# Stick-breaking iterations in two slices, with three PSUM banks for turned weights and one for outputs

## The reference

```python
def _stick_breaking(q, k, v, q_pos, k_pos):
    z = jnp.einsum('bqhd,bkhd->bhqk', q, k) * (SB_HEAD_DIM ** -0.5)
    causal = k_pos[None, :] < q_pos[:, None]
    log_keep = jnp.where(causal, jax.nn.log_sigmoid(-z), 0.0)
    after = lax.cumsum(log_keep, axis=3, reverse=True) - log_keep
    a = jnp.where(causal, jnp.exp(jax.nn.log_sigmoid(z) + after), 0.0)
    o = jnp.einsum('bhqk,bkhd->bqhd', a, v)
```

## Time and profile before

| | us |
|---|---|
| median of 3 runs | 1417.03 (1416.87 to 1417.48) |
| the profiled execution, its own time | 1415.79 |
| its span | 1414.0 |
| PE busy in the span | 1364.6 (97%) |
| DVE busy | 1000.3 (71%) |
| ACT busy | 624.1 (44%) |
| stick-breaking iterations 20 to 39 | about 436 to 582 |

### The profile page before, as it was taken

The page is one execution under the profiler, slowest core; times in us unless marked ns, Lnnn a source line. Parts: engine busy times, 40 slices in busy tenths (PEclk is TensorE's granted clock), DMA queues, the critical chain, the costliest instruction groups (busy, mean ns, idle before and its releaser), DMA issues. The chain is left out here.

```text
span 1414.0 us, 23804 instructions
## 1 busy us (share of the span) xinstructions
PE 1364.6 (97%) x9152; PEld 1195.7 (85%) x9152; DVE 1000.3 (71%) x1319; ACT 624.1 (44%) x1112; POOL 451.9 (32%) x412
## 2 busy tenths in 40 slices
PE   6999999989999999899789999999999999999997
PEld 5778888768888777688689999999999998788886
DVE  5896858598877999656677766666766567754466
ACT  6634333278887877323352222222222233533343
POOL 2133331010010000111164543544554454644344
PEclk9999999989999999999999999999999999999999
DMA  7265542455544555433234533444533448854554
GB/s 249 75 212 189 203 156 73 145 153 143 139 119 121 138 146 147 147 120 108 67 120 144 173 113 136 158 144 144 174 126 132 149 158 284 304 176 163 164 182 171
DMA packets 172200, 218.05 MB, mean 154 GB/s; under 512 B 19836, under 2 KB 110328, under 8 KB 170680
## 3 DMA queue, kind: packets, MB, share of 16 engines
q1 hardware_dynamic: 163416, 193.13, 41.9%
q0 software_dynamic: 3840, 12.58, 2.7%
q10 hardware_dynamic: 4832, 10.82, 2.1%
HBM read 152.98 MB, written 63.50 MB: 153 GB/s over the span
## 5 line engine op out<-in xcount | busy, mean ns | idle before, releaser
L792 PE MATMUL ps_proj<-shared 128*128 128x512 f32 x224 | 90.0, 402 | 2.4 <-DVE shared L546 1.5
L2605 ACT COPY aux<-ps_feed 128x544 f32<-128x544 f32 x22 | 13.5, 612 | 170.3 <-PE ps_feed L2926 170.3
L793 PE MATMUL ps_proj<-shared 128*128 128x512 f32 x224 | 87.9, 392 | 0.0
L794 PE MATMUL ps_proj<-shared 128*128 128x512 f32 x224 | 87.9, 392 | 0.0
L2555 POOL TENSOR_TENSOR ring_more<-staging,ring_more 128x512 fp32r<-128x512 f32 x45 | 69.5, 1548 | 56.5 <-ACT ring_more L2591 56.4
L2555 POOL TENSOR_TENSOR shared<-staging,shared 128x512 fp32r<-128x512 f32 x41 | 60.0, 1468 | 86.1 <-ACT shared L2591 86.1
L1408 ACT COPY aT<-ps_aT 128x512 f32<-128x512 f32 (+2 forms) x168 | 81.1, 526 | 10.7 <-PE ps_aT L1735 9.6
L1735 PE MATMUL ps_aT<-ident,z 128*128 128x128 f32 (+1 forms) x568 | 83.5, 280 | 1.9 <-DVE z L1580 1.7
L2819 DVE TENSOR_TENSOR blocks<-ps_feed,blocks 128x512 f32<-128x512 f32 x56 | 35.9, 681 | 67.1 <-PE ps_feed L2955 67.1
L1580 DVE TENSOR_TENSOR_SCAN z<-z,near 128x1024 f32<-128x1024 f32 (+7 forms) x64 | 81.4, 1335 | 0.0
L2924 PE MATMUL ps_feed<-shared,ring_more 128*128 128x272 f32 x264 | 76.6, 290 | 2.4 <-issue 2.4
(11 more groups left out here) (364 smaller groups left out, 4527.1 us busy)
## 6 DMA issues: line engine op xcount, KB each, us to landing
staging<-s_dram SPq DMA_DIRECT2D x50, 256.0 KB, 4.2
staging<-in_w_gate SPq DMA_DIRECT2D x11, 1024.0 KB, 7.8
blocks<-in_w_up SPq DMA_DIRECT2D x11, 1024.0 KB, 5.4
blocks<-in_w_down SPq DMA_DIRECT2D x11, 1024.0 KB, 9.8
t_dram<-blocks SPq DMA_DIRECT2D x11, 1024.0 KB, 3.9
s_dram<-blocks SPq DMA_DIRECT2D x11, 1024.0 KB, 5.2
w_raw<-in_w_in SPq DMA_DIRECT2D x10, 1024.0 KB, 6.5
staging<-in_cache_sb_v POOLq DMA_DIRECT2D x31, 256.0 KB, 3.2
```

The source lines that it names most:

```text
L792: nc.tensor.matmul(res, a_hi[:, k, cols], b_hi[:, k], start=start, stop=False)
L793: nc.tensor.matmul(res, a_hi[:, k, cols], b_lo[:, k], start=False, stop=False)
L794: return nc.tensor.matmul(res, a_lo[:, k, cols], b_hi[:, k], start=False, stop=(k == HK - 1))
L2605: nc.scalar.copy(two(first), bank(u, 0)).then_inc(first_done, 1)
```

## The change

In stick-breaking iterations (i >= 20) all engines use the slices `((0, 1, 2), (3, 4), ())`: three groups are turned in a row, then all products that are due follow in one row, then three score units; then two groups, their products and the rest of the units, and both pieces of preparation. The products run three groups behind instead of two. For this the four PSUM banks beside the ring are dealt out anew: three for turned groups and one for outputs in stick-breaking steps (differential ones keep two and two). A turned group then waits for the copy of the group three before, and the first product of a step for the output of the step just before. The ring for the scores keeps its four banks. No operation is added or removed.

```diff
-    RAW, RING, ZS, AT, LAG, POS = 6, 4, 4, 4, 2, 5
+    RAW, RING, ZS, AT, POS = 6, 4, 4, 4, 5
-    SLICES = ((0, 1), (2, 3), (4,))
+    DIFF_SLICES, SB_SLICES = ((0, 1), (2, 3), (4,)), ((0, 1, 2), (3, 4), ())
+    def slices(i):
+        return SB_SLICES if i >= SB0 else DIFF_SLICES
+    def lag(x):
+        return 2 if is_diff(x) else 3
     def pieces_of(i, s):
+        if i >= SB0:
+            return prep_at.get(i, ()) if s == 1 else ()
         return prep_at.get(i, ())[s - 1:s] if s else ()
+    def turned_bank(x, g):
+        G = grp0[x] + g
+        return G % 2 if is_diff(x) else (G - grp0[SB0]) % 3
+    def output_bank(x):
+        return 2 + x % 2 if is_diff(x) else 3
...
-        ps_aT = psum("ps_aT", [P, 2, 4, P])
-        ps_o = psum("ps_o", [P, 2, BANK])
+        ps_w = psum("ps_w", [P, 4, BANK])
...
-                if G >= 2:
-                    pe.wait_ge(a_copied, G - 1)
+                first = grp0[SB0]
+                if is_diff(x) or G < first + 2:
+                    if G >= 2:
+                        pe.wait_ge(a_copied, G - 1)
+                elif G == first + 2:
+                    pe.wait_ge(o_done, SB0 - 1)
+                else:
+                    pe.wait_ge(a_copied, G - 2)
...
-                        pe.wait_ge(o_done, x - 1)
+                        pe.wait_ge(o_done, x - 1 if is_diff(x) else x)
...
+            valued = upto = 0
             for i in iterations:
-                for s, slots in enumerate(SLICES):
+                for s, slots in enumerate(slices(i)):
                     turned_now = [j for j in slots if 0 <= i < NSTEP and j < len(groups(i))]
                     for j in turned_now:
                         turn(i, j)
-                    for j in turned_now:
-                        if grp0[i] + j >= LAG:
-                            values(grp0[i] + j - LAG)
-                    for j in slots:
-                        if i == NSTEP and j < LAG:
-                            values(len(owner) - LAG + j)
+                    if turned_now:
+                        upto = grp0[i] + turned_now[-1] + 1 - lag(i)
+                    elif i == NSTEP:
+                        upto = len(owner)
+                    while valued < upto:
+                        values(valued)
+                        valued += 1
                     for j in slots:
                         if 0 <= i + SCORE < NSTEP and j < len(units(i + SCORE)):
                             score(i + SCORE, j)
```

More of the change, by code:

```diff
@@ L1407, in collect @@
                 f = sum(m == P for _, _, _, _, m in bl)
-                last = nc.scalar.copy(aT[:, G % AT, 0:f], ps_aT[:, G % 2, 0:f])
+                ps = ps_w[:, turned_bank(x, g)].rearrange("p (k n) -> p k n", n=P)
+                last = nc.scalar.copy(aT[:, G % AT, 0:f], ps[:, 0:f])
                 if f < len(bl):
                     m = bl[f][4]
-                    last = nc.scalar.copy(aT[0:m, G % AT, f], ps_aT[0:m, G % 2, f])
+                    last = nc.scalar.copy(aT[0:m, G % AT, f], ps[0:m, f])
                 last.then_inc(a_copied, 1)
@@ L1420, in output @@
                     act.wait_ge(v_last_loaded[u % 2], 32 * ((u - ND) // 2 + 1))
-                o, ps = o_sb[:, x % 4], ps_o[:, x % 2]
+                o, ps = o_sb[:, x % 4], ps_w[:, output_bank(x)]
                 if is_sample(x) and is_diff(x):
@@ L1731, in turn @@
                     pe.wait_ge(ready, ready0[x] + 2 * r + h + 1)
-                if G >= 2:
-                    pe.wait_ge(a_copied, G - 1)
+                first = grp0[SB0]
[6 more added lines that the diff above has]
+                    pe.wait_ge(a_copied, G - 2)
+                ps = ps_w[:, turned_bank(x, g)].rearrange("p (k n) -> p k n", n=P)
                 for k, (_, _, _, at, m) in enumerate(groups(x)[g]):
-                    last = nc.tensor.transpose(ps_aT[0:m, G % 2, k], z(x, at, m), t["ident"][:, :])
+                    last = nc.tensor.transpose(ps[0:m, k], z(x, at, m), t["ident"][:, :])
                 last.then_inc(a_turned, 1)
@@ L1758, in values @@
                     val = v[u % 2][0:m, (NB if is_sample(x) else 0) + k]
-                    out = ps_o[:, x % 2]
+                    out = ps_w[:, output_bank(x)]
                     if is_diff(x):
```

## The result

The changed kernel takes 1422.95 us (1421.66 to 1424.89, 6 runs) against 1417.14 (1416.57 to 1417.95, 6 runs) of the kernel before on the same chip: a ratio of 1.0044 [1.0034, 1.0054], slower by 5.8 us. The profiled execution took 1421.66 us, its span is 1419.9. The prediction said 1422.2.

A forecast was written before the change was run, and what follows sets the result against it. PE, busy 97% of the span, was taken as the bound, with DVE close behind. DVE's last stretch 5.4 us later, less 0.3, plus 0.1 gave 1421.0 profiled; the median standing 1.24 higher, 1422.2 us, range 1417.6 to 1426.0.

The forecast's parts named there:

- The wait: In 14 prompt-scoring iterations PE's third score unit waits for ACT's sigmoids to free the first unit's banks, 0.8 to 1.1 us each.
- the 6 us under which I would have been wrong: Sign against the forecast: PE's idle time on scores under 6 us, where some 13 us was expected.
- The savings: Joined runs on PE save 0.14 (transposes) and 0.18 us (products) in each of 20 iterations, plus score-run ends.
- no wait to speak of: Rival: banks come free in time and only savings remain, 8.9 us on PE, of which DVE leaves part; 1412 us, 9%.
- The sum: Waits of 10.4 us less savings through iteration 32 bring PE 4.4 us later to iteration 33; the span grows by 5.2 us.
- the saving of 0.42: Per prompt-scoring iteration on PE: 0.32 us from joined transposes and products plus 0.10 for one end of a score run.
- The tail: DVE's last stretch, from the last preparation piece to the last scan, sets the stage's end and starts 5.4 us later.
- One output bank: A step's first product waits for the previous output; covered by scores, and in iterations 37 to 39 at worst 0.1 us each.
- The hole of 0.27 us: Wait in the transposes starting iteration 24, for an older group's copy; gone with three banks, the same taken for 29 and 34.
- The scans: Rival: DVE's scans come too late for the third group in iterations like 26, 31, 36; 2.8 us more, 1425.0 us, 14%.
- The clock: Rival: PE's clock falls to 1.2 GHz behind each of the 14 waits; 25 us more, 1447 us, 2%.

The follow-up runs named there:

- e2: The kernel before, with only the third score unit moved to join the first two in slice 0; 1425.76 us, ratio 1.0067.
- e1: The changed kernel, with the third score unit back in the second slice, behind the transposes and products of groups 3 and 4; 1415.08 us, ratio 0.9992.
- e3: The changed kernel, with the score units of each prompt step from step 23 on sorted by width, narrowest first; 1418.34 us, ratio 1.0013.
- e10: The kernel before, with only the new bank deal: three banks for turned groups, one for outputs in stick-breaking steps; 1416.48 us, ratio 0.9997.
- e5: The kernel of e1, with the rounding and remainder of the output weights moved from DVE to POOL; 1417.97 us, ratio 1.0008.
- e4: The changed kernel, with two banks for turned groups and two for outputs as before, products still three groups behind; 1434.04 us, ratio 1.0122.

## Why the prediction was right

**The wait, right.** Third units start 2.28 or 2.29 us after first ones of 512 (iterations 25, 26), and 1.89 where the first unit has 384 (23, 28; forecast 1.87). The sum of the idle marks is 11.2 us in 14 waits (13.4 by starts), all in the iterations and at the units that were named; the 6 us under which I would have been wrong were far off. e2 shows that the order of the units alone makes them, e1 that they go with it, e3 that their size follows the width of the first unit.

**The savings, right.** 12 transposes take 1.40 us (forecast 1.46), 20 products 1.24 (1.23). e1 is the kernel that has the savings without the wait: its stage is 2.24 us shorter. So they are there, but the rival "no wait to speak of" had the right reason against itself: of 8.9 us on PE most is not to be had, because DVE is next. It took half to two thirds as what remains, 5 us; a quarter (2.24 of 8.9) is what remained.

**The sum, 1.1 us short.** Through iteration 32 the change costs 5.10 us by lengths of iterations, against 4.4. By type of iteration (x mod 5 = 0, 1, 2, 3) the prediction gave 0.53, 0.70, 0.37 and 0.47 more for each with prompt scores, and 0.69 less for 24 and 29. Measured: 0.56 and 0.54 in 25 and 30 (but 0.12 in 20, the first of the stage), 0.87, 0.97 and 0.98 in 21, 26 and 31, 0.48, 0.48 and 0.47 in 22, 27 and 32, 0.48 in 23 and 28, and 0.67 and 0.65 less. The step that failed in size is the saving of 0.42, above all in the iterations with x mod 5 = 1, where it was 0.15 in 26 and 31. In 26 the wait is what was forecast, 1.12 (from 486.00 + 0.12 to 487.24); but the third unit's run had been followed at once by two small transposes of preparation before, which cost nothing extra at its end, so that no end was saved there, and the 12 transposes at the start took 1.51 us, 0.11 over those of iteration 25. I used the rows of iteration 25 for all, and 26 had another order behind its third unit. In 22, 27 and 32 the saving was 0.31: the sample step's products (L1764 before, L1788 after) gave 0.06 instead of 0.18. Against that stands luck of 0.4 in iteration 20, which nobody had forecast: with the longer lag 8 recorded products fewer are due there (28 instead of 36), and they come back behind the last transposes of the stage.

**The tail, right in kind.** DVE's last stretch sets the end: 34.03 us long in both. By the distance from iteration 20 it starts 6.06 us later, not 5.4, which is the same 0.7 as above. From the last scan to `mix` the sum had 0.2 less, and it is 0.2 more: that is the other 0.4 of the 1.1. "One output bank" was the other undersized term: nothing before iteration 37, as said, but 0.28 there and 0.39 at the last step, where I had at worst 0.1 each. e10, where the products are two groups behind, has neither.

**The rest.** The hole of 0.27 us is gone in the changed kernel and in e10 alike. The scans, a rival with 14%, cost 0.75 us at iteration 35 and 0.53 at 38, less in sum than the 1.7 before: PE's own waits give DVE its time. Once those go (e1), this rival's mechanism is the bound, at the third group of iteration 26 too (0.76 us). The clock was at 1.00 in both stretches. The Trainium skill (TensorE: Matmul & The Clock Gate, the section on depth-cycling) tells of a kernel whose clock oscillated with frequent short idles; 14 idle times of 0.6 to 1.0 us in 129 us (439 to 568) do not bring it down here. Right behind the stage, after PE idled 1.51 and 1.40 us (as it does there in the kernel before), the granted clock is 0.50 from 590.6 to 594.0 us in the changed kernel and 1.00 in the one before; that the change is the cause is not shown, since e3 has no such fall and e1 has one twice as long.

The profiled execution stood 1.3 us under the median in both kernels. So 1415.79 + 6.26 = 1422.05 would have been the exact sum for the profiled execution and 1423.3 for the median; measured were 1421.66 and 1422.95. So that the forecast of 1422.2 lies only 0.75 us off is in part luck: the stage was 1.1 us longer than its sum, and 0.4 of that was given back by the time before and behind it.

## What to carry to other kernels

Before you pull work of one kind together, ask what the work between was covering: count the buffers that the joined piece needs against the ring, and from the trace take how long after the first piece its buffer comes back. Here four banks against six meant 2.28 us until the first bank was free, against 1.0 to 1.5 us of work to fill them. Join only what has buffers for it (transposes and products, with a third bank), leave the other split (the scores), and then look for who is next, since a faster engine can hand most of its gain to waits for the one behind it, as PE did here to DVE (2.24 of 8.9 us were left in e1).

## What the hardware showed that I had not expected

- GpSimd and VectorE stop each other for whole instructions: 128x512 subtractions on POOL took 1.28 us alone, 3.2 in the mean and 15.59 at worst in e5, and DVE's four scans took 7.96 instead of 5.10. An engine that is idle is not free for work if it shares a way to memory with the critical one.
- A wait in the middle of a run can cost more than the idle mark says: 0.93 for 0.73 in e4, where the run is cut in two.
